# A two-block transformer kernel on one core: a new beginning, rope scores from stacked halves, and the last residual quarters turned by VectorE and ScalarE

## The chip, the core and the metric

The kernel runs on one core of a Trainium2 chip. TensorE (PE) multiplies, VectorE (DVE) and ScalarE (ACT) prepare its operands and take its results out of PSUM, GpSimd (POOL) does a few memsets, and SyncE (SP) issues all DMAs from one queue in program order. The metric is the device time in microseconds of one execution; the median of several runs counts.

## The reference, cut to what matters

256 tokens of width 2048 in float32 pass two attention layers and then a hybrid layer with an MLP:

```python
x  = residual_update(x, mixer_a(rms_norm(x, norm_pre[0]), ...), ...)      # stick-breaking attention
kv = shared_kv(x, ...)
x  = residual_update(x, mixer_b(rms_norm(x, norm_pre[1]), kv, ...), ...)  # attention with rope
# scores of mixer_b, per head: nope part (128 wide) + rope part (64 wide), k_rope shared by all heads
s = (einsum('bqhd,bkhd->bhqk', qn, k_nope) + einsum('bqhr,bkr->bhqk', qr, k_rope)) * scale
# the last layer: q, k, v, r, glr, pu = split(rmsnorm(h, norm1_w) @ w_in), h = meta tokens + x
h = h + mixed @ w_out
z = rmsnorm(h, norm2_w) @ mlp_w1
h = h + square(relu(z)) @ mlp_w2
```

Every large product is computed in two halves: a number is split into a rounded "hi" part (type fp32r) and the rest "lo", and hi\*hi + hi\*lo + lo\*hi is summed in PSUM.

## The kernel before

The work is a fixed list of stages (`plan`), each with chunks of output columns and units of weights. One unit is one 512 KB DMA into `raw`, which has 4 slots (`RING`). ACT rounds it into `whi` (`split_to`, L1140), DVE computes `wlo = raw - whi` (L1701), and PE uses both. SP loads unit u only once `lo_done` shows that DVE is through with unit u-4, and all loads stand in one queue: a wait in front of one holds all that come after. ACT and DVE work four units ahead of PE: in `along`, step `uu` of a chunk first splits unit `uu + 3` and only then runs the hooks given for `uu`. So what hangs on a hook comes after a split, on both engines. Below, the units are counted from a stage's start: unit 8 of stage `q2` is the first unit of the next stage, `k2`.

PE needs activations with the contraction on the partitions. There are two ways to turn them. PE can transpose 128x128 blocks into the banks `tp` (`turn`, L547), from which ACT takes hi (`hi_batch`, L1181) and DVE lo (`lo_batch`, L1742). Or a quarter (512 columns) is turned in the buffer `mov` without PE: DVE transposes 32x32 blocks (`blocks_turned`, L1758), in four bands; where the time is short, two of the bands are made from a copy that DVE flips in one go (`flipped`, L1749) and ACT moves (`bands_moved`, L1192). Then ACT takes hi of the quarter from `mov` (`hi_moved`, L1205) and DVE lo (`lo_moved`, L1775), which raises `split_lo`. `x1` to `x5` are the residuals as they are needed turned; `x4` feeds the last layer's input projection and `x5` its MLP. Of `x4` and `x5` quarters 0 to 2 go through `mov`, and PE turns the last quarter as two batches of 4 transposes in step 4 of the stage that needs it (`LAST`): stage `q2` (the queries of the last layer) for `x4`, the first chunk of `up0` (the MLP) for `x5`. The last quarter is needed from unit 6 on.

In step 7 of `q2` PE makes a row of inverse roots (`turn_rs`, L874 and L876), for which it waits on `rs_diag`. That comes from the hook `queries_norm` at step 5: ACT squares the last quarter of x and takes the root, DVE the reciprocal and the diagonal (L2147). After `q2` come the products `latents` (L886), then stage `k2`. SP loads the small gate weights `gw` between the loads of `q2` and those of `k2`, behind a wait on `x_done`. Buffer `gw2` lies on `mov`.

In the attention with rope, `scores(c)` makes the scores of two heads: float32 products of the nope parts (L804), then of the rope parts (L809), where each head's 64 rows are one half of the partitions of `qr` and `krT`. DVE turns the queries' rope part (`roped_queries`).

At the start, PE runs transposes that nobody uses (`fill`), 11 while the first inputs come and 22 before the first product; the order of the DMAs is x's first 256 columns, weight unit 0, x's next 256 columns, then x's second quarter ahead of weight unit 1, and so on.

Of the kernel before, what the change touches and what calls it, by code (L numbers as in the profile page):

```python
# [15 lines left out]
F32 = mybir.dt.float32  # L16
# [5 lines left out]
P = 128  # L22
# [4 lines left out]
CH = 512  # L27
# [27 lines left out]
FLIPPED = [("x1", 3), ("x3", 3)]  # L55
MOVED = [(name, c) for name, cs in (("x1", [3]), ("x2", [0, 1, 2]), ("x3", [3]), ("x4", [0, 1, 2]), ("x5", [0, 1, 2])) for c in cs]
# [89 lines left out]
def build(nc, w, const, out):  # L146
# [3 lines left out]
    with ctx:  # L150
# [76 lines left out]
        qr = sb("qr", [P, 2, SEQ], F32, r4 + 4 * KB)  # L227
        krT = sb("krT", [P, 2, SEQ], F32, r4 + 6 * KB)
# [51 lines left out]
        ident = const_of("ident")  # L280
        GC = {"pre0": 0, "pre1": 16, "kv": 32, "norm1": 48, "norm2": 64, "kvl": 80, "ql": 84, "gla": 88, "pool": 90}
# [5 lines left out]
        def sem(name):  # L287
            if name not in sems:
# [15 lines left out]
                 ("x4", [6, 7]), ("rsb", 1), ("qdec", 2), ("kend", 2),  # L304
                 ("vT", 4), ("kvM", 1), ("mixed", 4), ("x5", [6, 7])]
# [86 lines left out]
        def _(sp):  # L392
# [24 lines left out]
            for uu in range(s.units):  # L417
                if uu == 0:
                    c = slice(0, 2 * P)
                    sp.dma_start(x[:, :, c], x_rows(w["x"][0])[:, :, c]).then_inc(sem("x_first_in"), 16)  # L420
                elif uu < NCH:
                    c = slice(uu * CH, (uu + 1) * CH)
                    sp.dma_start(x[:, :, c], x_rows(w["x"][0])[:, :, c]).then_inc(sem(f"x_in{uu}"), 16)
                if uu == NCH:
                    for l in range(2):
                        sp.dma_start(psrc[:, l], x_rows(w["p"][l, 0])).then_inc(sem(f"p_in{l}"), 16)
                load(s, 0, uu)
                if uu == 0:
                    c = slice(2 * P, CH)
                    sp.dma_start(x[:, :, c], x_rows(w["x"][0])[:, :, c]).then_inc(sem("x_in0"), 16)  # L430
# [42 lines left out]
            sp.wait_ge(x_done, 16)  # L473
# [22 lines left out]
        def _(pe):  # L496
# [102 lines left out]
            pe.wait_ge(sem("ident_in"), 16)  # L599

# [16 lines left out]
            def columns_of(q, r=0, need=None, hooks={}):  # L617

                for uu in range(s.units):
# [6 lines left out]
                    pe.wait_ge(lo_done, u + 1 + r)  # L626
                    for two in ((0, 1), (2, 3)):
                        for k in range(s.kt):
                            kt, end = uu * s.kt + k, last and k == s.kt - 1
                            wc = [slice(k * CH + ct * P, k * CH + (ct + 1) * P) for ct in range(QT)]  # L630
                            for ct in two:
                                pe.matmul(tiles[q % 2][ct][:, :], whi[:, slot, wc[ct]], aT[:, kt, :, :].rearrange("p i t -> p (i t)"),  # L632
                                          start=first and k == 0, stop=False)
                            for ct in two:
                                mm = pe.matmul(tiles[q % 2][ct][:, 0:SEQ], wlo[:, slot, wc[ct]], aT[:, kt, 0, :], start=False, stop=end)  # L635
                                if end and ct < QT - 1:
                                    mm.then_inc(sem("qk_t"), 1)
# [159 lines left out]
            def scores(c):  # L797
# [8 lines left out]
                for o, qt, n in blocks:  # L806
                    for i in range(2):
                        rows = slice(i * ROPE, (i + 1) * ROPE)
                        mm = pe.matmul(xb[i][:, o:o + n], qr[rows, c % 2, qt * P:(qt + 1) * P], krT[rows, i, 0:n], start=False, stop=qt == 1)  # L809
                        if qt:  # L810
                            mm.then_inc(sem("attB_s"), 1)
# [68 lines left out]
            def latents():  # L880

                pe.wait_ge(tp_done, BATCH["x4", 7][0] + 1)
# [1570 lines left out]
```

## Time and profile before

| | us |
|---|---|
| median of 3 runs | 2068.93 |
| lowest, highest | 2066.84, 2070.9 |
| the profiled execution's own time | 2067.52 |
| its span | 2065.7 |
| PE busy in the span | 2053.3 |
| DVE busy | 1295.1 |
| ACT busy | 1093.6 |

The span is the time between the first and the last instruction of the profiled execution. In timeline rows the columns are the start, the time from the first start to the last end of a merged run of like instructions, engine, line, operation, output and inputs, shapes, the count, and in brackets idle time before it and what ended it. A matmul's own duration is longer than the distance to the next, since they overlap; the distance is what it costs.

### The profile page before, as it was taken

What the parts mean: (1) busy time and instruction counts of PE and PEld (TensorE: products, weight loads), DVE (VectorE), ACT (ScalarE), POOL (GpSimd) and SP (SyncE); (2) the same over time, 40 slices, a digit from 0 to 9 for tenths busy, and PEclk for the clock granted to TensorE, in tenths of its full rate; (3) what the DMA queues carried; (4) which work ended last, traced back from release to release, by engine and by line L of the source; (5) the groups of instructions that cost most, each with busy time, mean ns of one, the idle gap of its engine ahead of it and who ended that gap; (6) DMA issues with size and microseconds to landing.
All of it is one profiled execution on the core that took longest, in us unless ns stands there. A gap on an engine that the chain in (4) does not pass through costs nothing.

```text
span 2065.7 us, 27118 instructions
## 1 busy us (share of the span) xinstructions
PE 2053.3 (99%) x10736; PEld 1755.4 (85%) x10736; DVE 1295.1 (63%) x1676; ACT 1093.6 (53%) x1555; POOL 6.1 (0%) x12
## 2 busy tenths in 40 slices
PE   9999999999999999999999999999999999999998
PEld 8888888888898888888889988888888888888886
DVE  5555556557977677658955567966556556655554
ACT  6444566646566677546564355555435434434444
POOL 0000000000000000000000000000000000000000
PEclk9999999999999999999999999999999999999999
DMA  8666555555655545555645446665666666666664
GB/s 268 185 185 192 179 147 157 187 190 170 200 176 185 171 143 163 180 196 179 196 142 159 134 147 215 194 192 184 195 193 185 196 193 186 195 192 189 191 192 146
DMA packets 211101, 375.43 MB, mean 182 GB/s; under 512 B 13843, under 2 KB 48885, under 8 KB 210454
## 3 DMA queue, kind: packets, MB, share of 16 engines
q1 hardware_dynamic: 210982, 373.79, 58.3%
q8 instruction: 81, 1.33, 0.3%
q14 instruction: 38, 0.31, 0.0%
HBM read 371.64 MB, written 2.10 MB: 181 GB/s over the span
## 4 chain that ended last, share of the span: by engine, by line
PE 99%; ACT 0%; DMA 0%; DVE 0%; issue 0%; SPq 0%; ACTq 0%
PE acc L535 19%; PE acc L537 19%; PE acc L536 19%; PE acc L1079 6%; PE acc L632 3%; PE tp L1079 3%; PE xb L1079 3%; PE acc L1082 3%; PE acc L961 2%; PE acc L963 2%; PE acc L962 2%; PE tp L632 1%; PE xb L632 1%; PE acc L635 1%; PE xb L1082 1%; PE tp L1082 1%
## 5 line engine op out<-in xcount | busy, mean ns | idle before, releaser
L1701 DVE TENSOR_TENSOR wlo<-raw,whi 128x1024 fp32r<-128x1024 f32 x634 | 773.5, 1224 | 608.6 <-ACT whi L1140 606.9
L1140 ACT ACTIVATE whi<-raw 128x1024 fp32r<-128x1024 f32 x634 | 670.8, 1061 | 754.1 <-PE acc L537 432.3
L535 PE MATMUL acc<-whi,both 128*128 128x512 f32 (+1 forms) x976 | 376.5, 386 | 0.1
L537 PE MATMUL acc<-whi,both 128*128 128x512 f32 (+1 forms) x976 | 374.0, 383 | 0.0
L536 PE MATMUL acc<-wlo,both 128*128 128x512 f32 (+1 forms) x976 | 373.8, 383 | 0.0
L535 PEld LDWEIGHTS acc<-whi,both 128*128 128x128 f32 x976 | 183.2, 188 | 37.6 <-issue 2.7
L537 PEld LDWEIGHTS acc<-whi,both 128*128 128x128 f32 x976 | 183.2, 188 | 36.2
L536 PEld LDWEIGHTS acc<-wlo,both 128*128 128x128 f32 x976 | 183.3, 188 | 34.4
L1079 PE MATMUL acc<-bT,whi 128*128 128x512 f32 x512 | 160.8, 395 | 0.0
L535 PE MATMUL acc<-whi,bhi 128*128 128x512 f32 x384 | 150.1, 391 | 0.0
L537 PE MATMUL acc<-whi,blo 128*128 128x512 f32 x384 | 149.5, 389 | 0.0
L536 PE MATMUL acc<-wlo,bhi 128*128 128x512 f32 x384 | 149.4, 389 | 0.0
L1082 PEld LDWEIGHTS acc<-bT,wlo 128*128 128x128 f32 x512 | 96.2, 188 | 22.7
L535 PE MATMUL acc<-whi,aT 128*128 128x512 f32 x256 | 101.4, 396 | 0.0
L1082 PE MATMUL acc<-bT,wlo 128*128 128x256 f32 x512 | 100.6, 278 | 0.0
L537 PE MATMUL acc<-whi,aT 128*128 128x512 f32 x256 | 99.9, 390 | 0.0
L536 PE MATMUL acc<-wlo,aT 128*128 128x512 f32 x256 | 99.7, 389 | 0.0
L961 PE MATMUL acc<-lhi,whi 128*128 128x272 f32 x320 | 94.3, 295 | 0.0
L963 PE MATMUL acc<-lhi,wlo 128*128 128x272 f32 x320 | 92.8, 290 | 0.0
L962 PE MATMUL acc<-llo,whi 128*128 128x272 f32 x320 | 92.2, 288 | 0.0
L537 PEld LDWEIGHTS acc<-whi,blo 128*128 128x128 f32 x384 | 72.1, 188 | 14.9
L535 PEld LDWEIGHTS acc<-whi,bhi 128*128 128x128 f32 x384 | 72.1, 188 | 14.8
(401 smaller groups left out, 3149.9 us busy)
## 6 DMA issues: line engine op xcount, KB each, us to landing
raw<-in_mlp_w SPq DMA_DIRECT2D x256, 512.0 KB, 4.3
raw<-in_w_in_a SPq DMA_DIRECT2D x128, 512.0 KB, 3.8
raw<-in_w_ple_gate SPq DMA_DIRECT2D x64, 512.0 KB, 4.2
raw<-in_w_in SPq DMA_DIRECT2D x64, 512.0 KB, 3.9
raw<-in_w_in_b SPq DMA_DIRECT2D x40, 512.0 KB, 4.1
raw<-in_w_out_a SPq DMA_DIRECT2D x32, 512.0 KB, 4.2
raw<-in_w_out_b SPq DMA_DIRECT2D x32, 512.0 KB, 4.1
raw<-in_w_out SPq DMA_DIRECT2D x32, 512.0 KB, 4.2
```

The lines of the kernel that those rows point to most:

```text
L535: pe.matmul(o, hi[:, kt, tok], whi[:, slot, wc], start=start, stop=False)
L536: pe.matmul(o, hi[:, kt, tok], wlo[:, slot, wc], start=False, stop=False)
L537: mm = pe.matmul(o, lo[:, kt, tok], whi[:, slot, wc], start=False, stop=stop)
L632: pe.matmul(tiles[q % 2][ct][:, :], whi[:, slot, wc[ct]], aT[:, kt, :, :].rearrange("p i t -> p (i t)"), start=first and k == 0, stop=False)
L635: mm = pe.matmul(tiles[q % 2][ct][:, 0:SEQ], wlo[:, slot, wc[ct]], aT[:, kt, 0, :], start=False, stop=end)
L961: pe.matmul(o, whi[:, slot, wc], lhi[:, kt, :], start=first and k == 0, stop=False)
L962: pe.matmul(o, whi[:, slot, wc], llo[:, kt, :], start=False, stop=False)
L963: mm = pe.matmul(o, wlo[:, slot, wc], lhi[:, kt, :], start=False, stop=last and k == s.kt - 1)
L1079: pe.matmul(banks[ct][:, :], whi[:, slot, wc[ct]], bT[:, kt, :, :].rearrange("p i t -> p (i t)"), start=first and k == 0, stop=False)
L1082: mm = pe.matmul(banks[ct][:, 0:SEQ], wlo[:, slot, wc[ct]], x5hi[:, kt, :], start=False, stop=end)
L1140: act.activation(whi[:, u % RING, 0:n], raw[:, u % RING, 0:n], ACT.Copy).then_inc(hi_done, 1)
L1701: dve.tensor_tensor(wlo[:, u % RING, 0:n], raw[:, u % RING, 0:n], whi[:, u % RING, 0:n].bitcast(F32), ALU.subtract).then_inc(lo_done, 1)
```

## The change

Three things are changed. (1) The beginning: PE's first work is 7 float32 products of a zeroed buffer instead of 11 transposes; 2 and 9 fill transposes stand around the first turned batch instead of 22 after the second; the first weight unit is split in two halves, and PE may start on the first half; weight units 1 to 3 are loaded ahead of x's quarters 1 to 3, and `p` two units later. (2) The rope scores: `qrs` holds the rope part of one head as hi in its own 64 rows and lo in the other head's 64 rows; `krhi` holds the keys' hi in both halves, `krlo` their lo in one half; two fp32r products over all 128 rows replace one float32 product over 64. ACT and DVE make `qrs` (`queries_hi`, `queries_lo`) once per pair of heads. (3) The last quarters of `x4` and `x5` go through `flipped`, `bands_moved`, `blocks_turned`, `hi_moved` and `lo_moved` in stage `q2` and in the first chunk of `up0`; PE's 16 transposes there go. SP's wait ahead of the gate weights, whose buffer lies on `mov`, is now for `split_lo` of that quarter.

```diff
-FLIPPED = [("x1", 3), ("x3", 3)]
-MOVED = [... ("x4", [0, 1, 2]), ("x5", [0, 1, 2])) for c in cs]
+FLIPPED = [("x1", 3), ("x3", 3), ("x4", 3), ("x5", 3)]
+MOVED = [... ("x4", [0, 1, 2, 3]), ("x5", [0, 1, 2, 3])) for c in cs]
...
@@ sync @@
                 load(s, 0, uu)
-                if uu == 0:
-                    c = slice(2 * P, CH)
+                if uu < NCH:
+                    c = slice(uu * CH if uu else 2 * P, (uu + 1) * CH)
                     sp.dma_start(x[:, :, c], x_rows(w["x"][0])[:, :, c]).then_inc(sem(f"x_in{uu}"), 16)
...
             stage("q2")
-            sp.wait_ge(x_done, 16)
+            sp.wait_ge(sem("split_lo"), MOVED.index(("x4", 3)) + 1)
@@ tensor @@
-            pe.wait_ge(sem("ident_in"), 16)
-            fill(11)
+            pe.wait_ge(sem("consts_set"), 1)
+            for n in range(7):
+                pe.matmul(xb[n % 2][:, 0:P], zeros, zeros, start=True, stop=True)
+            pe.wait_ge(sem("ident_in"), 16)
...
-            for f in range(2):
-                turn("x0", f)
-            fill(22)
+            fill(2)
+            turn("x0", 0)
+            fill(9)
+            turn("x0", 1)
...
-                for o, qt, n in blocks:
-                    for i in range(2):
-                        rows = slice(i * ROPE, (i + 1) * ROPE)
-                        mm = pe.matmul(xb[i][:, o:o + n], qr[rows, c % 2, qt * P:(qt + 1) * P], krT[rows, i, 0:n], ...)
+                for i in range(2):
+                    for o, qt, n in blocks[::-1]:
+                        q = qrs[:, i, qt * P:(qt + 1) * P]
+                        pe.matmul(xb[i][:, o:o + n], q, krhi[:, 0:n], start=False, stop=False)
+                        mm = pe.matmul(xb[i][:, o:o + n], q, krlo[:, i, 0:n], start=False, stop=qt == 0)
...
-            product(S["q2"], 0, x4hi, x4lo, need="x4", hooks=join(turns("x4", LAST), {7: [turn_rs]}))
+            product(S["q2"], 0, x4hi, x4lo, need="x4", hooks={7: [turn_rs]})
...
@@ scalar @@
             for f in range(3):
                 hi_batch("x0", f, mhi, GC["pre0"])
+                if f == 0:
+                    act.wait_ge(raw_full[0], raw_count(0))
+                    for k, done in enumerate((sem("first_hi"), hi_done)):
+                        c = slice(k * CH, (k + 1) * CH)
+                        act.activation(whi[:, 0, c], raw[:, 0, c], ACT.Copy).then_inc(done, 1)
...
-            along(s, 0, join(his("x4", x4hi, GC["norm1"], LAST), {5: [queries_norm]}))
+            along(s, 0, join({q: [lambda q=q: bands_moved("x4", 3, q, 1)] for q in range(2)},
+                             {3: [lambda: hi_moved("x4", 3, x4hi, GC["norm1"])], 5: [queries_norm]}))
@@ vector @@
-            along(s, 0, join(los("x4", x4hi, x4lo, GC["norm1"], LAST), {5: [queries_norm], 7: [rs_out]}))
+            dve.wait_ge(x_done, 16)
+            flipped(x, 3, 1)
+            along(s, 0, join({q - 1: [lambda q=q: blocks_turned("x4", 3, q)] for q in (2, 3)},
+                             {3: [lambda: lo_moved("x4", 3, x4hi, x4lo, GC["norm1"])], 5: [queries_norm], 7: [rs_out]}))
...
+            dve.wait_ge(evac_dve, S["out2"].c0 + 4)
+            flipped(x, 3, 1)
...
-                        hooks = {} if q else join(los("x5", x5hi, x5lo, GC["norm2"], LAST), {4: [norm2_squared]})
+                        hooks = {} if q else join({q - 1: [lambda q=q: blocks_turned("x5", 3, q)] for q in (2, 3)},
+                                                      {3: [lambda: lo_moved("x5", 3, x5hi, x5lo, GC["norm2"])], 4: [norm2_squared]})
```

SP's queue from the last loads of the stage ahead through those of `q2` (`raw<-in_w_in 128x2x512`), the gate weights (`gw`) and the first loads of `k2` (`128x4x256`), before:

```order
L470 DMA graw<-in_w_in 128x8x16
L399 DMA raw<-in_w_ple_gate 128x2x512 [waits lo_done] x8
L399 DMA raw<-in_w_in 128x2x512 [waits lo_done] x8
L475 DMA gw_133<-in_gate_w_2 16x512 [waits x_done]
L475 DMA gw_133<-in_gate_w_2 16x512
L476 DMA gw_133<-in_gate_b 1x512
L399 DMA raw<-in_w_in 128x4x256 [waits lo_done] x40
```

And the same place of the changed kernel:

```order
L470 DMA graw<-in_w_in 128x8x16
L402 DMA raw<-in_w_ple_gate 128x2x512 [waits lo_done] x8
L402 DMA raw<-in_w_in 128x2x512 [waits lo_done] x8
L475 DMA gw_135<-in_gate_w_2 16x512 [waits split_lo]
L475 DMA gw_135<-in_gate_w_2 16x512
L476 DMA gw_135<-in_gate_b 1x512
L402 DMA raw<-in_w_in 128x4x256 [waits lo_done] x40
```

Nothing moved here; the semaphore of the wait that stands ahead of 40 weight loads did.

ACT in stage `q2`, before: the sigmoids of the stage ahead (L1397), the splits (`whi`) of units 3 to 7, hi of the last quarter (L1181), the split of unit 8, and the squares and the root of `queries_norm`:

```order
L1397 ACTIVATE stg<-acc 128x512
L1140 ACTIVATE whi<-raw 128x1024 [waits unit_used,raw_full3]
L1140 ACTIVATE whi<-raw 128x1024 [waits unit_used,raw_full0]
L1140 ACTIVATE whi<-raw 128x1024 [waits unit_used,raw_full1]
L1140 ACTIVATE whi<-raw 128x1024 [waits unit_used,raw_full2]
L1140 ACTIVATE whi<-raw 128x1024 [waits unit_used,raw_full3]
L1181 ACTIVATE lhi<-tp,gcol 128x256 [waits tp_full]
L1181 ACTIVATE lhi<-tp,gcol 128x256
L1181 ACTIVATE lhi<-tp,gcol 128x256 [waits tp_full]
L1181 ACTIVATE lhi<-tp,gcol 128x256
L1140 ACTIVATE whi<-raw 128x1024 [waits unit_used,raw_full0]
L1215 ACTIVATE xb,ssq<-x 128x512 [waits squares,x_done]
```

And of the changed kernel, from the split of unit 3 to the squares:

```order
L1147 ACTIVATE whi<-raw 128x1024 [waits unit_used,raw_full3]
L1199 ACTIVATE mov<-stg 32x2x128 [waits split_lo,flipped]
L1199 ACTIVATE mov<-stg 32x2x128 x3
L1147 ACTIVATE whi<-raw 128x1024 [waits unit_used,raw_full0]
L1199 ACTIVATE mov<-stg 32x2x128 x4
L1147 ACTIVATE whi<-raw 128x1024 [waits unit_used,raw_full1]
L1147 ACTIVATE whi<-raw 128x1024 [waits unit_used,raw_full2]
L1212 ACTIVATE lhi<-mov,gcol 128x256 [waits moved]
L1212 ACTIVATE lhi<-mov,gcol 128x256 x3
L1147 ACTIVATE whi<-raw 128x1024 [waits unit_used,raw_full3]
L1147 ACTIVATE whi<-raw 128x1024 [waits unit_used,raw_full0]
L1222 ACTIVATE xb,ssq<-x 128x512 [waits squares,x_done]
```

Eight band copies stand between the splits now, and the split of unit 8 (the last `raw_full0`, the first unit of `k2`) stands ahead of the squares as it did.

DVE in the same stage, from the update of x's last quarter (`x<-x,pp`) on, in the changed kernel; before, five `wlo` stood between that update and the four `llo` (L1742), with no transposes:

```order
L2027 TENSOR_TENSOR x<-x,pp 128x2x512 [waits evac_dve]
L1775 STREAM_TRANSPOSE stg<-x 128x512 [waits x_done]
L1775 STREAM_TRANSPOSE stg<-x 128x512
L1727 TENSOR_TENSOR wlo<-raw,whi 128x1024 [waits hi_done] x2
L1784 STREAM_TRANSPOSE mov<-x 32x2x128 x4
L1727 TENSOR_TENSOR wlo<-raw,whi 128x1024 [waits hi_done]
L1784 STREAM_TRANSPOSE mov<-x 32x2x128 x4
L1727 TENSOR_TENSOR wlo<-raw,whi 128x1024 [waits hi_done]
L1801 SCALAR_TENSOR_TENSOR llo<-mov,gcol,lhi 128x256 [waits split_hi]
L1801 SCALAR_TENSOR_TENSOR llo<-mov,gcol,lhi 128x256 x3
L1727 TENSOR_TENSOR wlo<-raw,whi 128x1024 [waits hi_done] x2
L1815 TENSOR_REDUCE ssum<-ssq 128x2 [waits squares]
```

Two large and eight small transposes stand between the update of x and `llo`.

## Rows read from the trace of the kernel before

**Rows 1.** The page, busy time of TensorE in the span.

```profile
PE 2053.3 (99%) x10736; PEld 1755.4 (85%) x10736; DVE 1295.1 (63%) x1676; ACT 1093.6 (53%) x1555; POOL 6.1 (0%) x12
```

**Rows 2.** The timeline, the first 11 us, TensorE and VectorE.

```profile
2.66 2.61 PE L603 MATMUL xb<-tab 128*128 128x128 f32 x11 [2.66 <-DMA tab<-tables]
...
7.70 0.66 PE L547 MATMUL tp<-tab,x 128*128 128x128 f32 x4 [1.17 <-DMA x<-in_x]
8.19 2.57 PE L603 MATMUL xb<-tab 128*128 128x128 f32 x22
8.45 1.23 DVE L1701 TENSOR_TENSOR wlo<-raw,whi 128x1024 fp32r<-128x1024 f32 x1
10.51 0.71 PE L632 MATMUL acc<-aT,whi 128*128 128x512 f32 x2
```

**Rows 3.** The timeline of TensorE, the first pair of heads with rope.

```profile
690.77 0.93 PE L809 MATMUL xb<-krT,qr 64*128 64x128 f32 x8
691.62 0.50 PE L535 MATMUL acc<-whi,both 128*128 128x512 f32 x1
```

**Rows 4.** The timeline of TensorE, fp32r products of 128 columns elsewhere.

```profile
361.62 0.22 PE L685 MATMUL tp<-tAhi,sums_of 128*128 128x128 f32 x1
...
361.79 0.39 PE L683 MATMUL tp<-tAhi,sums_of 128*128 128x384 f32 x1
```

**Rows 5.** The timeline of TensorE, around the transposes of x5.

```profile
1362.74 0.40 PE L1082 MATMUL xb<-bT,wlo 128*128 128x256 f32 x2
1362.98 1.04 PE L547 MATMUL tp<-tab,x 128*128 128x128 f32 x8
1363.77 0.70 PE L1079 MATMUL acc<-bT,whi 128*128 128x512 f32 x2
```

**Rows 6.** The timeline of TensorE in stage q2.

```profile
1042.62 0.40 PE L535 MATMUL acc<-whi,lhi 128*128 128x512 f32 x1
...
1045.38 1.03 PE L547 MATMUL tp<-tab,x 128*128 128x128 f32 x8
...
1054.63 0.39 PE L874 MATMUL tp<-diagM,tab 16*128 16x16 f32 x2
...
1058.28 0.28 PE L886 MATMUL xb<-lhi,gwT 128*32 128x272 f32 x1
```

**Rows 7.** The timeline of VectorE in stage q2.

```profile
1040.94 4.62 DVE L1701 TENSOR_TENSOR wlo<-raw,whi 128x1024 fp32r<-128x1024 f32 x4
...
1053.94 0.21 DVE L2147 TENSOR_SCALAR diagM<-tab,rs 16x16 f32<-16x16 f32 x1
```

**Rows 8.** The timeline of VectorE, the flip and one band of x3's last quarter.

```profile
947.74 1.30 DVE L1749 STREAM_TRANSPOSE stg<-x 128x512 f32<-128x512 f32 x2
...
954.35 1.79 DVE L1758 STREAM_TRANSPOSE mov<-x 32x256 f32<-32x256 f32 x4
```

**Rows 9.** The timeline of ScalarE, a band of x3 and hi of an x4 quarter.

```profile
949.07 1.70 ACT L1192 ACTIVATE mov<-stg 32x256 f32<-32x256 f32 x4 [1.29 <-DVE stg L1749]
...
1028.78 1.70 ACT L1205 ACTIVATE lhi<-mov,gcol 128x256 fp32r<-128x256 f32 x4
```

**Rows 10.** The timeline of VectorE, lo of an x4 quarter.

```profile
1030.53 1.67 DVE L1775 SCALAR_TENSOR_TENSOR llo<-mov,gcol,lhi 128x256 fp32r<-128x256 f32 x4
```

**Rows 11.** The timeline of SyncE, the gate weights and the next loads.

```profile
1042.60 0.93 SPq L475 DMA_DIRECT2D gw<-in_gate_w  x2
...
1043.89 17.88 SPq L399 DMA_DIRECT2D raw<-in_w_in  x8
```

**Rows 12.** DMA issues of 1042.0 to 1042.5 us: name, count, size, us to landing.

```profile
raw<-in_w_in SPq DMA_DIRECT2D x1, 512.0 KB, 3.8
```

**Rows 13.** The timeline of ScalarE, the split of unit 8.

```profile
1049.27 1.06 ACT L1140 ACTIVATE whi<-raw 128x1024 fp32r<-128x1024 f32 x1 [0.79 <-PE acc L537]
```

**Rows 14.** The timeline of VectorE, its first split in the MLP.

```profile
1353.87 1.22 DVE L1701 TENSOR_TENSOR wlo<-raw,whi 128x1024 fp32r<-128x1024 f32 x1
```

**Rows 15.** Busy time by stretch, with TensorE's granted clock behind POOL's column.

```profile
1068.10:1071.40 3.30, 3.30 (x15) 3.27 (x15) 0.00 (x0) 0.59 (x1) 0.00 (x0) 0.50 0.50 159
```

More of the change, by code:

```diff
@@ L625, in columns_of @@
                     slot, first, last = u % RING, uu == 0, uu == s.units - 1
[L626 to L637, printed above, removed]
+                    pairs, ks = ((0, 1), (2, 3)), range(s.kt)
+                    if need and first:
+                        steps = [(two, k) for k in ks for two in pairs]
+                        pe.wait_ge(sem("first_lo"), 1)
+                    else:
+                        steps = [(two, k) for two in pairs for k in ks]
+                        pe.wait_ge(lo_done, u + 1 + r)
+                    for n, (two, k) in enumerate(steps):
+                        if need and first and n == len(pairs):
+                            pe.wait_ge(lo_done, u + 1)
+                        kt, end = uu * s.kt + k, last and k == s.kt - 1
+                        wc = [slice(k * CH + ct * P, k * CH + (ct + 1) * P) for ct in range(QT)]
+                        for ct in two:
+                            pe.matmul(tiles[q % 2][ct][:, :], whi[:, slot, wc[ct]], aT[:, kt, :, :].rearrange("p i t -> p (i t)"),
+                                      start=first and k == 0, stop=False)
+                        for ct in two:
+                            mm = pe.matmul(tiles[q % 2][ct][:, 0:SEQ], wlo[:, slot, wc[ct]], aT[:, kt, 0, :], start=False, stop=end)
+                            if end and ct < QT - 1:
+                                mm.then_inc(sem("qk_t"), 1)
                     mm.then_inc(unit_used, 1)
@@ L1465, in queries_swapped, with queries_hi @@
                 m.then_inc(sem("q_swapped"), 1)
+            def queries_hi(j):
+                act.wait_ge(sem("q_turned"), j + 1)
+                if j:
+                    act.wait_ge(sem("attB_s"), 2 * j)
+                for i in range(2):
+                    rows = slice(i * ROPE, (i + 1) * ROPE)
+                    m = act.activation(qrs[rows, i, :], qr[rows, :], ACT.Copy)
+                m.then_inc(sem("q_hi"), 1)
             for j in range(2):
@@ L1498, in _ @@
                         queries_swapped(c + 1)
+                    if not query and uu % 4 == 2 and c + 1 < SLOTS:
+                        queries_hi(c + 1)
                 if c % 2:
@@ L1649, in _ @@
                     else:
-                        hooks = {} if q else join(his("x5", x5hi, GC["norm2"], LAST), {4: [x5_norm]})
+                        hooks = {} if q else join({q: [lambda q=q: bands_moved("x5", 3, q, 1)] for q in range(2)},
+                                                      {3: [lambda: hi_moved("x5", 3, x5hi, GC["norm2"])], 4: [x5_norm]})
                     if not q and not j:
@@ L1811, in _ @@
                 lo_batch("x0", f, mhi, mlo, GC["pre0"])
+                if f == 0:
+                    for k, (ready, done) in enumerate(((sem("first_hi"), sem("first_lo")), (hi_done, lo_done))):
+                        c = slice(k * CH, (k + 1) * CH)
+                        dve.wait_ge(ready, 1)
+                        dve.tensor_tensor(wlo[:, 0, c], raw[:, 0, c], whi[:, 0, c].bitcast(F32), ALU.subtract).then_inc(done, 1)
+                    ptr[0] = 1
                 split_to(f + 1)
@@ L2086, in roped_queries, with queries_lo @@
                 dve.wait_ge(sem("q_turning"), 2 * j + 2)
-                dve.tensor_tensor(qr[:, j % 2, :], qr[:, j % 2, :], qswap[:, :], ALU.add).then_inc(sem("q_roped"), 1)
+                dve.tensor_tensor(qr[:, :], qr[:, :], qswap[:, :], ALU.add).then_inc(sem("q_turned"), 1)
+            def queries_lo(j):
+                dve.wait_ge(sem("q_hi"), j + 1)
+                for i in range(2):
+                    rows, to = slice(i * ROPE, (i + 1) * ROPE), slice((1 - i) * ROPE, (2 - i) * ROPE)
+                    m = dve.tensor_tensor(qrs[to, i, :], qr[rows, :], qrs[rows, i, :].bitcast(F32), ALU.subtract)
+                m.then_inc(sem("q_roped"), 1)
             def scores_out(c):
@@ L2129, in _ @@
                         queries_out(c + 1, (*acc[0], tp[0]))
+                    if more and k == 3:
+                        roped_queries(c + 1)
                     if more and k == 4:
-                        roped_queries(c + 1)
+                        queries_lo(c + 1)
                     if not more and k == 2:
```

54 lines of the change are left out of this document (27 added, 27 removed).

## The prediction, made before the changed kernel ran

> **What bounds the kernel now.** The page comes first: TensorE is busy 2053.3 us of a span of 2065.7, 99% [rows 1]. So an engine beside it costs nothing until it makes TensorE wait, and two things count: which instructions PE loses or gains, and whether its next operands still come in time. Then the timeline of the beginning shows the 10.5 us before the first product [rows 2], that of one pair of heads the price of the rope scores [rows 3, 4], and those of stage `q2` on all engines how early each operand of the last layer is ready [rows 6 to 13]. The reader should see in the latter that the margins are small: x's last quarter is complete only in `q2`, since DVE turns to its next split at 1040.94 [rows 7], when PE is in unit 2 of 8 (unit 3 starts at 1042.62 [rows 6]).
>
> **The beginning.** Before, the first product starts at 10.51, behind 22 fill transposes from 8.19 on, although `wlo` of unit 0 is ready at 8.45 + 1.23 = 9.68 [rows 2]. The second batch of x can't be turned ahead of its DMA, which lands at 7.69; its queue position stays, so the batch ends at about 8.2, and that is the floor. The other input, the first half of `wlo`, comes half a `wlo` and half a `whi` (0.61 + 0.53) earlier than 9.68, at 8.5, and up to 0.5 earlier if the first batch is turned at the full clock. The start is at 8.2 to 8.6: 1.9 to 2.3 us gained, I take 2.1. Weight unit 1 now lands ahead of x's second quarter, which PE needs only after the 2.8 us of unit 0, so the order is kept without a new wait. Bounds: 1.0 (the clock rises later, half of 2.8 us of work more at half speed) and 2.4. The fills matter for the clock. The 11 transposes at 2.66 stand 0.21 us apart and the 22 at 8.19 stand 0.11 apart [rows 2], two levels of the clock, and until 7.70 PE had run almost nothing but transposes. The Trainium skill (TensorE: Matmul & The Clock Gate, Part 4: PE-mode transpose) says that transposes don't count as activity for the clock; by that rule the new float32 products would raise it earlier and the old fills not at all. The rows contradict it, and the sum doesn't use it.
>
> **The rope scores.** Before: 8 records per pair of heads in 691.62 - 690.77 = 0.85 us, the two heads side by side in the two halves of the array [rows 3]; the product behind them is late by some 0.1 more. After: 4 fp32r products of 256 columns and 4 of 128. Two of 256 take 0.24 [rows 5], two of 128 take 361.79 - 361.62 = 0.17 [rows 4]: 0.48 + 0.34 = 0.82, against 0.95. The bounds of the small ones are 0.06 and 0.12 each, so per pair -0.25 to 0; times 8 pairs -2.0 to 0, I take 0.1 each, so -0.8. The Trainium skill (TensorE: Matmul & The Clock Gate, LDWEIGHTS) gives columns / 1.2 ns for a weight load, 107 ns for these; an estimate from that page, 8 x 107 ns = 0.86 us, would make the gain 0.7 us in all. The extra work of ACT (two copies of 64 rows) and DVE (two subtractions) per pair has a slot of six weight units to hide in. `roped_queries` moves one step ahead and ends well before the next scores; I expect no wait.
>
> **x5's last quarter.** PE loses 8 transposes: 1363.77 - 1362.98 = 0.79, and 0.08 more on the product behind [rows 5]: -0.9. What replaces them is off PE if it is ready for unit 6. Unit 4 would start at 1362.98, unit 6 two units of 2.79 later at 1368.6. DVE is free at 1353.87 [rows 14]: flip 1.3 [rows 8] to 1355.2; the split of unit 3 to 1356.4; ACT's two bands and its two splits in between (1.7 [rows 9] and 1.06 each) go from 1355.2 to 1360.7; DVE: split 4 at 1358.0 to 1359.2 (ACT's split for it comes behind the first band), band to 1361.0, split 5 to 1362.3, band 1.79 [rows 8] to 1364.1; ACT's hi 1.70 [rows 9] to 1365.8; DVE's lo 1.67 [rows 10] to 1367.5. That is 1.1 us before the need. Hidden.
>
> **x4's last quarter: the first wait.** The same chain in `q2` starts much later against PE. PE's need before: unit 3 at 1042.62, the transposes at 1045.38, `turn_rs` at 1054.63 between units 6 and 7, `latents` at 1058.28 [rows 6]; unit 6 at 1051.7. DVE is free at 1040.94 [rows 7]. Step by step: flip (1.30 [rows 8]) to 1042.3; split of unit 3 to 1043.5, so PE starts it 0.9 late, at 1043.5. ACT: first band 1042.4 to 1044.1, split 4 to 1045.1, second band to 1046.8, splits 5 and 6 to 1048.8. DVE: split 4 1045.2 to 1046.4, band to 1048.2, split 5 to 1049.5, band to 1051.3. PE, without its transposes: unit 4 at 1046.4, unit 5 at 1049.5, ready for unit 6 at 1052.3. ACT's hi 1051.3 to 1053.0, DVE's lo to 1054.7. PE waits 2.4 us and starts unit 6 at 1054.8, 3.1 later than before, the saved transposes already counted.
>
> **The second wait.** SP's queue stands on `split_lo` of this quarter until 1054.7; before it passed at 1042.60 [rows 11]. Behind the three gate DMAs comes the load of unit 8, the first of `k2`: issue 1043.89 - 1042.60 = 1.3 later [rows 11], at 1056.0, landing 3.8 later [rows 12] at 59.8 (all in 1000s). ACT, in order, has the split of unit 8 ahead of the squares of `queries_norm`, and those end in `rs_diag`. Before, from the start of that split to the end of the diagonal passed 1053.94 + 0.21 - 1049.27 = 4.9 us [rows 7, 13]: now 1064.7. PE wants `turn_rs` when unit 6 is done, at 1057.6. It stands 7.1 us. The 3 other loads of `k2` queue behind DVE and ACT only, and PE has unit 7 and `latents` (1058.28 - 1054.63 = 3.6 and 3.9 us) in which four slots fill; no third wait. `latents` starts at 1064.7 + 3.65 = 1068.35 instead of 1058.28: +10.0 us for the stage as a whole. Bounds: a load landing between 3.5 and 5 us makes this 9.7 to 11.2. If ACT squared first, it would be 3.1.
>
> **The clock behind it.** After such a pause the granted clock should fall to 1.2 GHz. Before, it stood at 0.50 for 3.3 us in the middle of dense work [rows 15], and at the start PE worked at half speed from 2.66 to beyond 6.5 [rows 2]. Half speed for 3.3 to 5 us costs 1.7 to 2.5 us; I take +2.0. Below, 0 (the pause might not lower it); above, 5 (if `latents`, which fills only 32 of the array's columns, keeps it low until `k2`).
>
> **The sum.** -2.1 - 0.8 - 0.9 + 10.0 + 2.0 = +8.2 us on the profiled execution's own 2067.5 (span 2065.7 and 1.8 around it): 2075.7. The median of the runs shown is 1.4 above that execution: 2077.1. I forecast 2077.
>
> **Rivals.**
> - *Both waits are hidden* (6%). This ends on the other side. If DVE and ACT run their parts in time, the change is worth -2.1 - 0.8 - 0.9 - 0.9 (x4's transposes) = -4.7: 2064.2. For it speaks that the same scheme of flip and bands runs for x1 and x3 while PE stays 99% busy [rows 1]; against it that there the flip comes well ahead of its stage, while here x is complete only 1.7 us before unit 3. It decides by one point: whether `lo_moved` ends before 1051, ten microseconds after x; the steps above add up to 13.8.
> - *Only the first wait* (6%). Should the load of unit 8 not pass behind `split_lo` in time to matter, or `turn_rs` find its diagonal, `q2` costs +3.1 and no clock: -2.1 - 0.8 - 0.9 + 3.1 = -0.7, 2068.2, no change. Against it stand the two order listings: the load is behind the wait, the squares behind the split.
> - *The clock stays low through `latents`* (9%): 3 us more, 2080.
> - *The beginning costs instead of gaining* (3%), when the clock comes up late: 2079.
>
> My forecast with the two waits has 76%, in its own range of 2073.5 to 2080. The range that should hold the time 8 times in 10 reaches a little to both sides: 2071.5 to 2081. A measurement can't tell less than 0.2%, 4.1 us, from no change, so same is 2064.8 to 2073.1. Faster by more 5%, same 9% (the second rival, and the low edge of the forecast), slower 86%.
>
> **What the profile would show.** Right, if PE's waits list a wait of about 2 to 3 us on `llo` of L1801 at unit 6 of `q2` and one of about 7 us at `turn_rs`, with SP standing on DVE for 10 us ahead of `gw`, ACT waiting for the DMA of the split of unit 8, and a stretch of half clock behind. The first product would start near 8.3; the rope products of a pair would take about 0.8; no wait in `up0`. Wrong, if PE goes through `turn_rs` without a pause, or if the squares run before the split of unit 8.

## The result and the profile after

| | us |
|---|---|
| before, median of 8 runs beside it | 2069.26 (2066.84 to 2070.9) |
| after, median of 8 runs | 2075.18 (2073.57 to 2077.06) |
| ratio, 95% interval | 1.0032 [1.0022, 1.0041] |
| span of the profiled execution after | 2072.0 (before 2065.7) |

The change makes the kernel slower: by 0.32% by the ratio, and by 5.9 us (0.29%) by the medians. Forecast were 2077 and a range of 2071.5 to 2081. Two executions further down (one of e7's kernel, 3441.87 us, and one of the kernel before beside it, 3446.52 us) ran at a mean granted clock of 0.556 and are left out of the ratios.

The page after, its first part; TensorE has 24 instructions fewer than in [rows 1]:

```profile
span 2072.0 us, 27142 instructions
...
PE 2052.3 (99%) x10712; PEld 1757.6 (85%) x10712; DVE 1312.3 (63%) x1715; ACT 1106.5 (53%) x1588; POOL 6.1 (0%) x12
```

TensorE is busy 1.0 us less and the span is 6.3 us longer: the time went into waits. The five longest waits of TensorE in the kernel after (us in all, times, longest):

```profile
PE tp L883 <- DVE diagM L2191: 5.6, 1, 5.6
PE acc L535 <- DVE llo L1801: 2.2, 1, 2.2
PE tp L547 <- DMA x<-in_x: 1.1, 2, 0.7
PE xb L604 <- DVE eps L1829: 1.1, 1, 1.1
PE acc L535 <- DVE wlo L1727: 0.8, 1, 0.8
```

The first, second and fifth are in `q2`; the other two are in the beginning. The timeline of TensorE there, and then through `q2`:

```profile
1.07 3.22 PE L604 MATMUL xb<-mov 128*128 128x128 f32 x14 [1.07 <-DVE eps L1829]
...
6.99 0.66 PE L547 MATMUL tp<-tab,x 128*128 128x128 f32 x4 [0.74 <-DMA x<-in_x]
7.94 0.70 PE L641 MATMUL acc<-aT,whi 128*128 128x512 f32 x2 [0.29 <-DVE wlo L1843]
...
1039.97 0.47 PE L535 MATMUL acc<-whi,lhi 128*128 128x512 f32 x1 [0.83 <-DVE wlo L1727]
...
1051.21 0.50 PE L535 MATMUL acc<-whi,lhi 128*128 128x512 f32 x1 [2.20 <-DVE llo L1801]
...
1061.41 0.60 PE L883 MATMUL tp<-diagM,tab 16*128 16x16 f32 x2 [5.61 <-DVE diagM L2191]
...
1066.92 0.28 PE L895 MATMUL xb<-lhi,gwT 128*32 128x272 f32 x1
```

The first product starts at 7.94 instead of 10.51 [rows 2]; the latter turns out to be an early one (see the beginning, further down). In `q2` stand three waits that [rows 6] doesn't have. The chain behind the last and longest goes over three engines. VectorE first:

```profile
1036.16 1.23 DVE L2027 TENSOR_TENSOR x<-x,pp 128x1024 f32<-128x1024 f32 x1
1037.42 1.30 DVE L1775 STREAM_TRANSPOSE stg<-x 128x512 f32<-128x512 f32 x2
...
1049.48 1.67 DVE L1801 SCALAR_TENSOR_TENSOR llo<-mov,gcol,lhi 128x256 fp32r<-128x256 f32 x4 [0.52 <-ACT lhi L1212]
...
1061.14 0.22 DVE L2191 TENSOR_SCALAR diagM<-tab,rs 16x16 f32<-16x16 f32 x1
```

SyncE (the gate weights, where [rows 11] has 1042.60):

```profile
1051.18 0.79 SPq L475 DMA_DIRECT2D gw<-in_gate_w  x2
```

And ScalarE (the split of unit 8, a square and the root):

```profile
1056.48 1.06 ACT L1147 ACTIVATE whi<-raw 128x1024 fp32r<-128x1024 f32 x1 [6.09 <-DMA raw<-in_w_in]
1057.44 0.58 ACT L1222 ACTIVATE xb<-x 128x512 f32<-128x512 f32 x1
...
1060.21 0.30 ACT L1228 ACTIVATE root<-ssum,eps 128x2 f32<-128x2 f32 x1
```

x is complete at 1036.16 + 1.23 = 1037.39, the last `llo` ends at 1051.15, SP passes at 1051.18, ScalarE gets unit 8 at 1056.48 after 6.09 us without work, and only then squares x, which has been complete for 20 us; the diagonal follows at 1061.14 + 0.22. From x complete to `latents` took 1058.28 - 1041.03 = 17.25 us before (the x update there ended at 1041.03) and takes 1066.92 - 1037.39 = 29.53 now: +12.3 us. [rows 13] has the same split at 1049.27, and the diagonal at 1053.94 [rows 7].

Last, the busy time by stretch after, TensorE's granted clock behind POOL's column: unit 6, the first stretch of the second wait, unit 7, and the products behind `latents`, which begin with three float32 products for the gates (L908, from 1073.90; the expectations below call them the gate logits).

```profile
1051.20:1055.80 4.60, 4.59 (x12) 3.30 (x12) 1.08 (x1) 0.00 (x0) 0.00 (x0) 0.63 0.47 145
1055.80:1058.60 2.80, 0.00 (x1) 0.00 (x0) 1.03 (x1) 2.09 (x4) 0.00 (x0) 1.00 1.10 362
...
1061.40:1065.60 4.20, 4.19 (x13) 3.57 (x14) 2.71 (x3) 1.34 (x2) 0.00 (x0) 0.51 0.37 117
...
1074.00:1083.00 9.00, 9.00 (x56) 6.91 (x56) 2.45 (x2) 5.62 (x7) 0.00 (x0) 1.00 0.19 58
```

Unit 6 takes 4.6 us at a mean of 0.63, most of it at 1.2 GHz; before, unit 6 took 1054.63 - 1051.7 = 2.9 us. And the stretch of half clock of [rows 15] is gone: behind the same gate products the clock stays at 1.00.

### The profile page after: what moved, and what is told of

The parts are those of the page before. It is cut to its first block, busy times and chain, and to the rows that moved or that the text cites. A ratio compares the mean times of both kernels' runs of the same rounds, so it can differ in the third digit from the quotient of the medians.

```text
span 2072.0 us, 27142 instructions
## 1 busy us (share of the span) xinstructions
PE 2052.3 (99%) x10712; PEld 1757.6 (85%) x10712; DVE 1312.3 (63%) x1715; ACT 1106.5 (53%) x1588; POOL 6.1 (0%) x12
## 4 chain that ended last, share of the span: by engine, by line
PE 98%; DMA 1%; ACT 1%; DVE 1%; issue 0%; SPq 0%; ACTq 0%
PE acc L535 19%; PE acc L536 19%; PE acc L537 19%; PE acc L1086 6%; PE xb L1086 3%; PE tp L1086 3%; PE acc L1089 3%; PE acc L641 3%; PE acc L970 2%; PE acc L972 2%; PE acc L971 2%; PE tp L641 1%; PE xb L641 1%; PE tp L1089 1%; PE xb L1089 1%; PE acc L644 1%
```

## The experiments

The theory: nearly all of the loss is `x4`'s last quarter in `q2`, as a first wait of PE for `llo` and a second that is not caused by the new work as such, but by SP's wait ahead of `k2`'s loads together with ScalarE's order (split of unit 8 ahead of the squares). The rivals: the loss sits in the beginning or the rope scores, or the second wait has only one cause, the lateness of `llo`, whatever the queues do.

**x4's last quarter back on TensorE** (e1), the rest of the change kept:

```diff
-FLIPPED = [..., ("x4", 3), ("x5", 3)]       # MOVED likewise: x4 has quarters 0 to 2
+FLIPPED = [..., ("x5", 3)]
...
-            sp.wait_ge(sem("split_lo"), MOVED.index(("x4", 3)) + 1)
+            sp.wait_ge(x_done, 16)
...
-            product(S["q2"], 0, x4hi, x4lo, need="x4", hooks={7: [turn_rs]})
+            product(S["q2"], 0, x4hi, x4lo, need="x4", hooks=join(turns("x4", LAST), {7: [turn_rs]}))
... (the hooks of ScalarE and VectorE and the wait of `latents` as in the kernel before)
```

> The changed kernel, with the last quarter of x4 turned by PE again as before (new beginning, rope scores and x5's quarter kept). My theory (SP's queue stands on split_lo ahead of k2's first load, and ACT has that unit's split ahead of the squares): all waits of PE in q2 go (0.8, 2.2 and 5.6 us) and the low clock behind them (about 4 us lost), 0.9 us of transposes come back. Against the kernel before: -2.6 (beginning), -1.1 (scores), -0.9 (x5), together -4.6 us, a ratio of 0.9978, and no wait on llo or diagM. Rival (the losses lie in the rope part or the beginning, such as a clock that falls more often): it stays above the kernel before, ratio 1.001 or more.

Measured: 2061.84 us (2061.52 to 2063.72), ratio to before 0.9974 [0.9963, 0.9984], span 2059.9. The waits of TensorE in it, all in the beginning:

```profile
PE xb L604 <- DVE eps L1828: 1.1, 1, 1.1
PE acc L641 <- DVE wlo L1842: 0.8, 1, 0.8
PE acc L641 <- DVE rsA L1874: 0.3, 1, 0.3
PE tp L547 <- DMA x<-in_x: 0.3, 1, 0.3
```

So the other parts gain, and this one costs 2072.0 - 2059.9 = 12.1 us of span, which is the +12.3 of the stage within 0.2. This is the fastest version of all, faster than both kernels.

**Only x4's last quarter** (e4): the kernel before with the `q2` part of the diff and nothing else.

```diff
-FLIPPED = [("x1", 3), ("x3", 3)]            # and MOVED
+FLIPPED = [("x1", 3), ("x3", 3), ("x4", 3)]
... (the hooks of q2 on the three engines and SP's wait, as in the change)
```

> The kernel before with only the x4 part of the change (quarter through mov, SP's wait on split_lo). My theory: q2 loses 12.3 us from x's update to latents as in the changed kernel; if the half clock behind the gate logits (1.7 us) goes as it did there, +10.6, else +12.3 us: ratio 1.0051 to 1.0060, waits on wlo 0.8, llo 2.2, diagM 5.6 us. Rival (the parts interact, for instance the earlier arrival in q2 makes the margins): well under +9 us.

Measured: 2081.24 us (2079.35 to 2082.99), ratio 1.0061 [1.0044, 1.0077]. TensorE in `q2`:

```profile
1057.04 0.50 PE L535 MATMUL acc<-whi,lhi 128*128 128x512 f32 x1 [2.17 <-DVE llo L1776]
...
1067.39 0.60 PE L874 MATMUL tp<-diagM,tab 16*128 16x16 f32 x2 [7.31 <-DVE diagM L2148]
```

Here unit 6 ran at the full clock and the second wait is 7.3 us instead of 5.6. From the start of unit 6 to `turn_rs` it is 10.35 us here and 1061.41 - 1051.21 = 10.20 after: the same. The half clock in unit 6 is hidden, since the diagonal, not TensorE, sets when `turn_rs` starts. By the ratio the edit alone costs 0.61%, 12.6 us, just above the expected range. In its trace x is complete at 1042.00 + 1.23 = 1043.23 and `latents` starts at 1073.71, 30.48 us against 17.25: +13.2, some 0.9 more than after, since the clock was back at full only at 1073.2.

**SP's wait behind three loads of k2** (e2). The gate weights' wait and DMAs stand behind units 0 to 2 of `k2`; ScalarE's order is untouched.

```diff
             stage("q2")
+            for uu in range(3):
+                load(S["k2"], 0, uu)
             sp.wait_ge(sem("split_lo"), MOVED.index(("x4", 3)) + 1)
             ... (the three gate DMAs)
-            for name in ("k2", "v2", "pu", "r2", "pool"):
+            load(S["k2"], 0, 3)
+            stage("k2", 1)
+            for name in ("v2", "pu", "r2", "pool"):
```

> The changed kernel with SP's wait for split_lo and the three gate DMAs moved behind the loads of the first three units of k2. My theory: the 5.6 us wait at turn_rs goes (under 0.5 us left) and with it the low clock of 1058 to 1066 us (2 us), the waits of 0.8 and 2.2 us stay. Against the changed kernel -7.5 us; if the half clock behind the gate logits comes back as before, -6. Ratio to the kernel before 0.9985 to 1.0005. Rival (ACT and DVE are simply too slow for the added work, the queue doesn't matter): turn_rs still waits over 4 us.

**The norm ahead of the split of unit 8** (e3). `queries_norm` at step 4 instead of 5 on ScalarE and VectorE; SP is untouched.

```diff
-                             {3: [lambda: hi_moved(...)], 5: [queries_norm]}))
+                             {3: [lambda: hi_moved(...)], 4: [queries_norm]}))
-                             {3: [lambda: lo_moved(...)], 5: [queries_norm], 7: [rs_out]}))
+                             {3: [lambda: lo_moved(...)], 4: [queries_norm], 7: [rs_out]}))
```

> The changed kernel with SP's queue as it is, but the hook with squares, root and diagonal one step earlier on ACT and DVE, ahead of the split of k2's first unit. My theory: the load of unit 8 is as late as now (ACT waits for it some 5 us), but nothing that PE needs stands behind it: turn_rs waits under 0.5 us, and unit 8 is split by about 1059 us, ahead of the end of latents. Same time as the kernel with the gate loads moved back, within 2 us. Rival (the late load alone starves k2, whatever the order on ACT): the wait only moves from turn_rs to k2's first product, 2 us or more, and the time stays within 2 us of the changed kernel.

Measured: e2 2066.71 us (2065.35 to 2068.01), ratio 0.9992 [0.9982, 1.0002]; e3 2066.58 us (2064.59 to 2068.05), ratio 0.9991 [0.9982, 1.0001]. e2's profile is 2072.0 - 2065.7 = 6.3 us shorter than that of after, as expected for a profile in which the half clock behind the gate products stands again (it does, from 1069.0 on). The timeline of TensorE in e2:

```profile
1050.99 0.50 PE L539 MATMUL acc<-whi,lhi 128*128 128x512 f32 x1 [2.17 <-DVE llo L1805]
...
1055.52 0.39 PE L887 MATMUL tp<-diagM,tab 16*128 16x16 f32 x2
```

`turn_rs` has no wait in front of it. Unit 6 takes 1055.52 - 1050.99 = 4.5 us here, for the clock fell in it. The timeline of TensorE in e3:

```profile
1051.13 0.50 PE L535 MATMUL acc<-whi,lhi 128*128 128x512 f32 x1 [2.18 <-DVE llo L1801]
...
1054.19 0.39 PE L883 MATMUL tp<-diagM,tab 16*128 16x16 f32 x2
```

And the timeline of ScalarE in e3, a square, the root and the split of unit 8:

```profile
1050.22 0.58 ACT L1222 ACTIVATE xb<-x 128x512 f32<-128x512 f32 x1
...
1052.99 0.30 ACT L1228 ACTIVATE root<-ssum,eps 128x2 f32<-128x2 f32 x1
1056.57 1.06 ACT L1147 ACTIVATE whi<-raw 128x1024 fp32r<-128x1024 f32 x1 [3.28 <-issue]
```

Unit 8 is as late as after (1056.57), and it no longer matters. Each edit alone takes the second wait away and leaves the first: the wait needs both causes, the load that stands behind `split_lo` and the squares that stand behind that load's split. "Late `llo`, whatever the queues do" fell. In e3, from x complete at 1037.31 to `latents` at 1057.80 it is 20.5 us, +3.2 against 17.25: the first wait's price, with no loss of clock.

**Only the beginning** (e5) and **only the rope scores** (e6), each the kernel before with that part of the diff.

```diff
-            fill(11)
+            for n in range(7):               # e5, with the new order of loads and fills
+                pe.matmul(xb[n % 2][:, 0:P], zeros, zeros, start=True, stop=True)
...
```

```diff
-                mm = pe.matmul(xb[i][:, o:o + n], qr[rows, ...], krT[rows, i, 0:n], ...)
+                pe.matmul(xb[i][:, o:o + n], q, krhi[:, 0:n], ...)          # e6
+                mm = pe.matmul(xb[i][:, o:o + n], q, krlo[:, i, 0:n], ...)
```

> The kernel before with only the new beginning. My theory: first product near 7.9 to 8.3 us instead of 10.5, nothing else changes: -2.3 to -2.6 us, ratio 0.9988. The half clock behind the gate logits may or may not come (1.7 us either way). Rival: part of the earlier start is lost again in the first eight units, where operands come later than PE wants them: under 1.5 us is left at the end of the first chunk.

Measured: 2065.06 us (2063.26 to 2065.93), ratio 0.9984 [0.9975, 0.9993]: 3.4 us by the medians, more than expected. The rival fell, for the first scores with rope start at 686.62 instead of 689.37, so 2.75 us are kept. The first product of e5:

```profile
8.31 0.70 PE L639 MATMUL acc<-aT,whi 128*128 128x512 f32 x2 [0.25 <-DVE wlo L1830]
```

Why the medians say more than that: the kernel before starts later in other executions. Its fills and first product in its second profile (e9):

```profile
8.19 4.52 PE L603 MATMUL xb<-tab 128*128 128x128 f32 x22
12.46 0.71 PE L632 MATMUL acc<-aT,whi 128*128 128x512 f32 x2
```

The 22 fills, which all stand ahead of the first product, take 12.46 - 8.19 = 4.27 us here and 2.32 in [rows 2]: most of them still run at half the pace. Five profiles have the old beginning, and their first scores start at 689.37 (before), 690.22 (e11), 690.80 (e9), 691.01 (e6) and 691.56 (e4). The seven with the new one (after, e10, e1, e12, e2, e3, e5) lie between 686.62 and 687.10. By the middle values the new beginning is worth 690.80 - 686.93 = 3.9 us, and by [rows 2] only 2.4.

> The kernel before with only the stacked rope scores. My theory: each of 8 pairs of heads takes 0.13 to 0.15 us less on PE, no wait on q_roped: -1.1 us by the trace from the first to the last pair, ratio 0.9995, too little for the times alone. Rival (the chain over ScalarE and back to VectorE makes PE or the score evacuation late): a wait on qrs or on krlo, 0 or more us.

Measured: 2066.46 us (2064.66 to 2068.71), ratio 0.9994 [0.9985, 1.0003], which by itself can't be told from no change. The trace can: from the first scores to the last there are seven slots and 826.62 - 691.01 = 135.61 us, before 826.00 - 689.37 = 136.63: 0.146 us a pair, 1.2 for all eight. The first pair in e6:

```profile
691.01 1.47 PE L806 MATMUL xb<-knT,qn 128*128 128x128 f32 x8
692.13 0.47 PE L811 MATMUL xb<-krhi,qrs 128*128 128x256 f32 x1
692.44 0.28 PE L812 MATMUL xb<-krlo,qrs 128*128 128x256 f32 x1
692.55 0.22 PE L811 MATMUL xb<-krhi,qrs 128*128 128x128 f32 x1
692.62 0.27 PE L812 MATMUL xb<-krlo,qrs 128*128 128x128 f32 x1
...
693.19 0.45 PE L537 MATMUL acc<-whi,both 128*128 128x512 f32 x1
```

No wait for `qrs` is in its trace.

**What raises the clock at the start**: the new beginning alone, with 7 transposes behind the identity's DMA in place of the 7 zero products (e7), and with neither these nor the fills (e8).

```diff
-            pe.wait_ge(sem("consts_set"), 1)
-            for n in range(7):
-                pe.matmul(xb[n % 2][:, 0:P], zeros, zeros, start=True, stop=True)
             pe.wait_ge(sem("ident_in"), 16)
+            fill(7)                  # e7; e8 has no fill at all, here or around turn("x0", 0)
```

> The kernel of the new beginning alone, but its 7 float32 products of zeros, which start at 1.1 us, are replaced by 7 transposes behind the wait for the identity at 2.7 us. My theory: PE's activity starts 1.6 us later, so the clock rises later; the first turned batch takes 1.1 instead of 0.6 us and the first product starts up to 0.5 us later, at 8.0 to 8.6, at the full clock: +0.2 to +0.8 us against the new beginning alone. Rival (the rule that transposes raise no clock): the clock stays at half until several us of real products have run, first product spacing 0.46 us for 3 us or more, +2 us or more.

> The new beginning alone, with neither products of zeros nor any of the 11 unused transposes; only the gains, x's first two batches and the products run. My theory: PE is hardly active before 7.9 us, so the first 3.5 to 5 us of products run at half clock: +1.7 to +2.5 us against the new beginning alone. Rival (the clock rises by itself or by the few real transposes, the fills are for nothing): within 0.5 us of it.

Measured: e7 2064.05 us (2063.76 to 2066.15), ratio 0.9984 [0.9975, 0.9994]; e8 2065.58 us (2064.75 to 2067.23), ratio 0.9991 [0.9982, 1.0]. The first 9 us of TensorE in e7:

```profile
2.67 1.76 PE L599 MATMUL xb<-tab 128*128 128x128 f32 x7 [2.67 <-DMA tab<-tables]
...
5.05 1.06 PE L545 MATMUL tp<-tab,x 128*128 128x128 f32 x4
5.91 1.30 PE L599 MATMUL xb<-tab 128*128 128x128 f32 x9
8.02 0.66 PE L545 MATMUL tp<-tab,x 128*128 128x128 f32 x4 [0.81 <-DMA x<-in_x]
8.78 0.70 PE L637 MATMUL acc<-aT,whi 128*128 128x512 f32 x2
```

And in e8:

```profile
8.62 1.11 PE L545 MATMUL tp<-tab,x 128*128 128x128 f32 x4 [2.89 <-DMA x<-in_x]
9.39 1.20 PE L634 MATMUL acc<-aT,whi 128*128 128x512 f32 x2
```

The same four transposes take 1.06 and 0.66 us in e7: the clock rose in between, with nothing but transposes behind it. Zero products and transposes are worth the same, within what the two medians can tell (2065.06 and 2064.05); the expected loss of 0.2 to 0.8 us shows in the trace alone (first scores at 687.11 against 686.62 in e5). The Trainium skill (TensorE: Matmul & The Clock Gate, Part 4: PE-mode transpose) says that the full clock doesn't engage for transposes, the rule that the prediction weighed. This trace speaks against it.

Without fills (e8) the first products still run at half the pace (1.20 against 0.70 us), and its first scores start at 690.07, 3.4 us later than in e5; 1.2 of that is x's second batch, which could be turned at 8.62 instead of 7.41. But by the medians e8 costs only 0.5 us against e5, less than the 1.7 to 2.5 expected and as much as the rival allowed. So the fills raise the clock, and what that is worth in time is not settled: 0.5 by the medians, more by this one profile.

**The stretch of half clock behind the gate products** is in the first profile of before and not in that after. Both kernels, unchanged, were profiled again, and e1's too.

> The kernel before, unchanged, profiled a second time. Theory A (the stretch of half clock behind the gate logits, 1068.1 to 1071.4 in the first profile, belongs to single executions): it may be absent here; the execution without it is 1.5 to 3 us shorter. Theory B (it belongs to the kernel's order of instructions, so the change removed it): it stands here again, within 1 us of its place, and the span is 2065 to 2067.

> The kernel before, unchanged, profiled a third time. As for its second profile: theory A has the stretch of half clock behind the gate logits in some of the three and not in others, theory B in all three.

> The changed kernel, unchanged, profiled a second time. Theory A (where the clock falls differs from execution to execution): the half clock behind the first wait of q2 or that behind the gate logits differs from the first profile; with unit 6 at the full clock the second wait is near 7.1 us instead of 5.6, with the sum of unit 6 and the wait the same 10 us. Theory B (the order sets it): 5.6 us again, no fall behind the gate logits, span 2071.8 to 2072.1.

> The changed kernel with x4's last quarter turned by PE, profiled a second time; its times fell into two groups, 2061.5 to 2062.0 and 2063.5 to 2063.7. Theory A: the groups are executions without and with a stretch of half clock behind the gate logits, so a time near 2062 goes with no stretch and one near 2063.6 with one of some 3 us. Theory B: it never has that stretch, and the groups have another cause.

Measured: before 2069.02 and 2068.37 us, after 2074.09, e1's kernel 2061.64. Busy time by stretch, before in its second profile:

```profile
1070.00:1073.30 3.30, 3.30 (x18) 3.30 (x18) 0.00 (x0) 0.28 (x1) 0.00 (x0) 0.55 0.53 159
```

And after in its second profile, unit 6 and unit 7:

```profile
1051.50:1055.90 4.40, 4.40 (x12) 3.22 (x12) 0.99 (x1) 0.00 (x0) 0.00 (x0) 0.61 0.48 142
...
1061.60:1066.00 4.40, 4.14 (x13) 3.59 (x14) 2.91 (x5) 1.59 (x2) 0.00 (x0) 0.53 0.40 126
```

The fall behind the gate products is in three of three profiles of before, in neither of after, and in neither of e1's kernel; the second wait after is 5.8 us again. That speaks against chance alone, as theory A had it, but doesn't rule it out. The order of the instructions at that place is the same in all kernels, e6 differs from before only in the rope scores and shows no fall, and e2 and e4 do show one. What decides it stays open.

The times fall into two groups, some 1 to 3 us apart, in after (2073.6 to 2073.9 and 2076.5 to 2077.1), in e1 to e5, in e7 and in e8. The cause isn't shown, but the record has a hint. In e3, e5 and e7 every execution of the lower group has a mean granted clock of 0.999, and every one of the upper group 0.998 or 0.997. The profiles of e2 (2067.52) and e4 (2082.99) fell in an upper group and have the fall behind the gate products; those of after, e1, e3, e5 and e7 fell in a lower group and have none. An estimate: 3.3 us at half speed lower the mean over 2065 us by 0.0008 and cost 1.65 us. So the groups may well be executions with and without that stretch, which is theory A after all. Against it stands e8's profile, in the upper of that kernel's two groups (2066.75) and without a fall.

## Why the prediction was right

Its steps against the traces:

| step | predicted | measured |
|---|---|---|
| first product | 8.2 to 8.6 | 7.94 (8.31 in e5, 8.77 in the second profile after) |
| beginning | -2.1 | -2.4 (-3.9 by the middle of all profiles) |
| rope scores | -0.8 | -1.2 |
| x5; ready ahead of its use by | -0.9; 1.1 | -0.9 (no wait); 0.8 |
| unit 3 late, wait at unit 6 | 0.9, 2.4 | 0.8, 2.2 |
| wait at `turn_rs` | 7.1 | 5.6 (7.3 in e4) |
| `q2` with the clock behind it | +12.0 | +12.3 |
| half clock behind the gate products | not spoken of | -1.65 (an estimate; only between the first two profiles) |
| sum | +8.2 | +6.15 by these rows; +6.3 by the spans, +5.9 by the medians |

- *The mechanism* was right, in both halves. From x to the last `llo` the steps added up to 13.8 us, and it took 1051.15 - 1037.39 = 13.8. Of the second wait's two causes e2 takes away one and e3 the other, and the wait goes each time.
- *The second wait* was too long by 1.5 us in the kernel after, and its sum right, since I had put the fall of the clock only behind the second pause. It falls already in unit 6, after the first wait of 2.2 us, and there the wait hides it; then it falls again.
- *The beginning*: the scores of the first pair start at 686.93 instead of 689.37, 2.4 us sooner. The term took 10.51 from one profile for the start of the kernel before; that was its earliest of five, and the others have 11.89 to 12.67. So by all profiles the term is 3.9 instead of 2.1: what was left out is that the 22 old fills themselves often run at half the pace. Left out too is the landing of x's second batch: it was turned at 6.99 in the first profile after, at 7.41 in e5, 8.02 in e7 and 8.36 in the second after, with the order of the DMAs the same.
- *The rope scores*: nope and rope products with the product behind them took 689.39 - 686.93 = 2.46 us instead of 2.6. The prices were read rightly: two small products take 688.64 - 688.47 = 0.17, as in [rows 4]. The prediction's own figures, 0.82 against 0.95, give 0.13 a pair and -1.0 in all; it took 0.1 and -0.8. From the first rope product to the next weight product it is 689.11 - 688.05 = 1.06, of which the first product alone takes 0.30. The estimate by the Trainium skill (TensorE: Matmul & The Clock Gate, LDWEIGHTS), 8 x 107 ns = 0.86 us a pair, lies below that. The trace's own weight loads there last 187 to 192 ns each (L818, L819), and as they overlap, neither figure is the price of a product.
- *x5*: the flip starts only at 1361.11, for VectorE came free 7.2 us later than in [rows 14], as TensorE did; `lo` ends at 1373.18 + 1.68 = 1374.86 and unit 6 starts at 1375.67. VectorE's last `bT` of x5 and TensorE's unit 6, from the timelines after:

```profile
1373.18 1.68 DVE L1801 SCALAR_TENSOR_TENSOR bT<-mov,gcol,bT 128x256 fp32r<-128x256 f32 x4 [0.53 <-ACT bT L1212]
```

```profile
1375.67 0.62 PE L1086 MATMUL acc<-bT,whi 128*128 128x512 f32 x2
```

- *What was mis-sized.* Between the first two profiles the forecast of +8.2 stands against +6.3. The largest part of the difference is the clock: half speed for 3.3 us in [rows 15] cost about 1.65 us of the profile before, and I read it only as a sign of what a pause does, not as time that can come and go. With the beginning (-0.3) and the rope scores (-0.4) that makes -2.35, and +0.3 in `q2`: 2.05 of the 8.2.
- *Luck*: by the medians the forecast is 1.9 us too high, nearly the same, but not for the same reason. The forecast added 1.4 us, by which the median before lies above its profile. In e9 and e11 such an excess (1.5 and 0.9 us) is the late start: their first scores start 1.43 and 0.85 us later than in the first profile, which the new beginning takes away. After, the median lies 1.4 above its profile as well, but because half of its executions are in the upper group of times. With 3.9 for the beginning and no row for the half clock the terms add up to -3.9 - 1.2 - 0.9 + 12.3 = +6.3, against +5.9 by the medians.

The four rivals fell: both waits showed, the second as well; the clock stood at 0.51 until 1065.60 and was back at full before `latents` at 1066.92; and the beginning gained.

## What to carry to other kernels

Moving work off a busy engine pays only where the result is due later than the replacement takes: here the chain from x to `llo` is 13.8 us long and the first use 10.7 away (1051.7 - 1041.0), while for `x5` the same chain has 0.8 us to spare. A semaphore wait that is put ahead of small loads holds every load behind it in that queue; ask which of them another engine has ahead of something urgent. Either cure (small loads later, or the urgent work ahead of the split) gives back some 7.5 us by the medians beside the kernel before (8.3 to 8.5 by the ratios), and here leaving the quarter on TensorE is better still by 5. Read a term from more than one profile where the clock is still rising: the start of the kernel before varied by 2.2 us between five.

## What the runs showed of the hardware

- The clock fell after a pause of only 2.2 us ([2.20 <-DVE llo]) in both profiles after and in e2, and not after the same pause in e3 and e4 (unit 6 took 1054.19 - 1051.13 = 3.1 us in e3 and 4.5 in e2, both without a wait behind it). So the same pause has two prices. The Trainium skill (TensorE: Matmul & The Clock Gate, Part 1, HAM oscillation) tells of kernels that lose the clock at each wait for a DMA; the traces here show a fall behind a wait of 2.2 us for another engine as well, and that it doesn't come each time.
- At the start the clock of the same program rises at different times: the first four transposes of x took 0.62 us after and 1.03 us in e1, which have the same beginning. The Trainium skill (TensorE: Matmul & The Clock Gate, Part 1, What's actually happening) says that the number of products at the low clock varies from run to run, and the traces agree. The granted clock doesn't show it: it reads 1.00 from 2.70 to 5.00 in the profile before, where the fills stand 0.21 us apart, twice the 0.11 of later. That it is the clock is inferred from the spacing.
- Three float32 products of 33 rows and 512 columns (6 records in 2.9 us, no pause) stand ahead of a fall to half clock in 5 of the 14 profiles (before, e9, e11, e2, e4), and ahead of none in the other nine.
